# High weights on both input halves in one 512-column matmul, for the gate and up projections of a two-layer macaron encoder

## The reference, cut to what matters

```python
def swiglu(x, w_gate, w_up, w_down):
    return (jax.nn.silu(x @ w_gate) * (x @ w_up)) @ w_down

for l in range(DEPTH):                      # DEPTH = 2
    x = x + 0.5 * swiglu(rms_norm(x, ffn1_norm[l]), ...)   # 1024 -> 2816 -> 1024
    ...                                     # attention, gated recurrence, S5 on one projection
    x = x + 0.5 * swiglu(rms_norm(x, ffn2_norm[l]), ...)
```

## Time and profile before

| | |
|---|---|
| median of 3 runs (lowest to highest) | 1073.03 us (1072.99 to 1074.38) |
| the profiled execution's own time | 1073.09 us |
| its span in the trace | 1071.3 us |
| busy: PE / PEld / DVE / ACT / POOL | 98% / 96% / 61% / 47% / 20% |
| mean granted TensorE clock | 0.998 |
| the chain that ended last, PE's share | 90% |

### The profile page before, as it was taken

How to read it: one execution, slowest core, us unless ns; L and a number is a source line. 1 busy time by engine, 2 the same in 40 slices (tenths; PEclk the granted TensorE clock), 3 DMA queues, 4 the chain that set the end, 5 groups by cost and what they waited for, 6 DMA issues and landing times.

```text
span 1071.3 us, 21293 instructions
## 1 busy us (share of the span) xinstructions
PE 1053.6 (98%) x8990; PEld 1032.1 (96%) x8990; DVE 654.3 (61%) x807; ACT 505.5 (47%) x590; POOL 210.4 (20%) x296
## 2 busy tenths in 40 slices
PE   8899999999999999999999999999999999999998
PEld 7899999999988999999999999999998899999998
DVE  4567666788743556555566666667976355555554
ACT  5555434555543743343464743347445445434332
POOL 3005998100000100000010089941000010000000
PEclk9999999999999999999999999999999999999999
DMA  7545455434222464555556445453432155455541
GB/s 291 214 157 196 162 198 189 158 120 158 84 114 92 184 232 161 196 170 187 192 180 232 170 183 182 171 196 119 159 119 80 79 196 197 164 191 188 184 175 40
DMA packets 26828, 178.37 MB, mean 167 GB/s; under 512 B 3120, under 2 KB 4144, under 8 KB 5776
## 3 DMA queue, kind: packets, MB, share of 16 engines
q1 hardware_dynamic: 25632, 173.03, 44.7%
q10 hardware_dynamic: 1008, 4.05, 1.1%
q0 software_dynamic: 128, 0.44, 0.1%
HBM read 176.46 MB, written 1.05 MB: 166 GB/s over the span
## 4 chain that ended last, share of the span: by engine, by line
PE 90%; DVE 4%; ACT 2%; DMA 1%; issue 1%; POOL 1%; SPq 0%; DVEq 0%; ACTq 0%; POOLq 0%
PE ps L786 26%; PE ps L787 26%; PE ps L788 26%; PE ps L1147 5%; PE ps L978 2%; DVE lo L1178 1%; ACT hi L556 1%; DMA raw<-stream 1%; PE ps L939 1%; POOL sumsq L413 1%; PE ps L1043 0%; PE ps L1039 0%; DVE sc L1559 0%; PE ps L1000 0%; SPq L340 0%
## 5 line engine op out<-in xcount | busy, mean ns | idle before, releaser
L1178 DVE TENSOR_TENSOR lo<-raw,hi 128x2048 fp32r<-128x2048 f32 x130 | 303.8, 2342 | 291.4 <-ACT hi L556 291.4
L786 PE MATMUL ps<-xg_hi,hi 128*128 128x256 f32 x1408 | 400.5, 284 | 5.2 <-DVE lo L1178 4.9
L787 PE MATMUL ps<-xg_lo,hi 128*128 128x256 f32 x1408 | 399.2, 283 | 0.0
L788 PE MATMUL ps<-xg_hi,lo 128*128 128x256 f32 x1408 | 399.1, 283 | 0.0
L556 ACT ACTIVATE hi<-raw 128x2048 fp32r<-128x2048 f32 x130 | 247.2, 1907 | 252.6 <-PE ps L788 220.6
L786 PEld LDWEIGHTS ps<-xg_hi,hi 128*128 128x128 f32 x1408 | 270.9, 192 | 5.9 <-DVE lo L1178 5.1
L787 PEld LDWEIGHTS ps<-xg_lo,hi 128*128 128x128 f32 x1408 | 271.0, 192 | 0.2
L788 PEld LDWEIGHTS ps<-xg_hi,lo 128*128 128x128 f32 x1408 | 271.0, 192 | 0.0
L786 PE MATMUL ps<-act_hi,hi 128*128 128x256 f32 x704 | 199.6, 284 | 4.1 <-DVE act_lo L1216 4.1
L787 PE MATMUL ps<-act_lo,hi 128*128 128x256 f32 x704 | 199.2, 283 | 0.0
L788 PE MATMUL ps<-act_hi,lo 128*128 128x256 f32 x704 | 199.2, 283 | 0.0
(11 more groups left out here) (298 smaller groups left out, 1285.0 us busy)
## 6 DMA issues: line engine op xcount, KB each, us to landing
raw<-stream SPq DMA_DIRECT2D x160, 1024.0 KB, 4.8
par<-params ACTq DMA_DIRECT2D x2, 1463.0 KB, 6.2
raw<-stream SPq DMA_DIRECT2D x8, 256.0 KB, 7.0
rows<-stream SPq DMA_DIRECT2D x2, 1024.0 KB, 6.9
x<-xT ACTq DMA_DIRECT2D x4, 256.0 KB, 6.3
out<-x SPq DMA_DIRECT2D x8, 128.0 KB, 2.0
con<-consts POOLq DMA_DIRECT2D x1, 321.5 KB, 6.6
mask<-masks POOLq DMA_DIRECT2D x1, 112.0 KB, 6.3
```

Source lines behind the costliest of these rows:

```text
L786: pe.matmul(acc, w_hi, a_hi, start=start, stop=False, skip_group_check=True)
L787: pe.matmul(acc, w_hi, a_lo, start=False, stop=False, skip_group_check=True)
L788: return pe.matmul(acc, w_lo, a_hi, start=False, stop=stop, skip_group_check=True)
L1178: v.tensor_tensor(lo[slot][:, :], raw[slot][:, :], hi[slot][:, :].bitcast(F32), ALU.subtract).then_inc(lo_written, 1)
```

## The change

`hi*xg_hi` and `hi*xg_lo` become one matmul of 512 columns on a joint tile `xg` that holds both halves side by side, so its 512 sums fill a bank: the first 256 columns are the high part, the last 256 the rest. `lo*xg_hi` stays a matmul of 256 columns and adds to the first half. Now a block's gate sums take banks 6 and 7 and its up sums banks 4 and 5, so there is one set, and step i waits for `gated(i)` to have read block i, where it waited for `gated(i-1)`. ACT copies the second halves out of PSUM (into `silu` and `act` as scratch), DVE adds them to the first halves and multiplies by `rstd` in place. Block 0 of each FFN keeps the old form in banks 4 and 5; so does down. The four pieces below are `gate_up` and `step` on PE, the head of ACT's `gated`, and DVE's `gated`.

```diff
-                def gate_up(half, n, slot, b, between=lambda: None):
+                def gate_up(n, slot, b, between=lambda: None):
                         for k in range(KT):
                             w = k * 256 + m * P
-                            last = three(bank(b + m)[:, half * T:(half + 1) * T], hi[slot][:, w:w + P],
-                                         lo[slot][:, w:w + P], xg_hi[:, k, :], xg_lo[:, k, :],
-                                         k == 0, k == KT - 1)
+                            pe.matmul(bank(b + m), hi[slot][:, w:w + P], xg[:, k, :, :].rearrange("p s t -> p (s t)"),
+                                      start=k == 0, stop=False, skip_group_check=True)
+                            last = pe.matmul(bank(b + m)[:, 0:T], lo[slot][:, w:w + P], xg_hi[:, k, :],
+                                             start=False, stop=k == KT - 1, skip_group_check=True)
...
-                    pe.wait_ge(gu_read, f * ITERS + i + 1)
-                    gate_up(0, n, 2, 4 + 2 * g, lambda: row_sums(norm, False, 3) if head and first else None)
-                    gate_up(1, n + 1, 0, 4 + 2 * g)
+                    pe.wait_ge(gu_read, f * ITERS + i + (1 if first else 2))
+                    gate_up(n, 2, 6, lambda: row_sums(norm, False, 3) if head and first else None)
+                    if first:
+                        pe.wait_ge(gu_read, f * ITERS + i + 2)
+                    gate_up(n + 1, 0, 4)
...
+                    if folded:
+                        e.wait_ge(units_done, n0 + i * 3 + 1 + RING)
+                        e.wait_ge(act_lo_ready, f * ITERS + i)
+                        for b, rest in ((6, silu), (4, act)):
+                            e.activation(rest[:, :, :], bank(b, 2).rearrange("p (m s t) -> p m s t", m=2, s=2)[:, :, 1, :],
+                                         ACT.Copy).then_inc(rest_copied, 1)
...
+                    v.wait_ge(rest_copied, (f * (ITERS - 1) + i) * 2 - 1)
+                    v.tensor_tensor(gate[:, :, :], of_gate[:, :, 0, :], silu[:, :, :], ALU.add
+                                    ).then_inc(gate_summed, 1)
+                    v.wait_ge(rest_copied, (f * (ITERS - 1) + i) * 2)
+                    v.tensor_tensor(up[:, :, :], of_up[:, :, 0, :], act[:, :, :], ALU.add).then_inc(gu_read, 1)
+                    v.wait_ge(gate_summed, f * (ITERS - 1) + i)
+                    v.tensor_tensor(gate[:, :, :], gate[:, :, :], wide, ALU.mult).then_inc(gate_scaled, 1)
+                    v.wait_ge(gu_read, f * ITERS + i + 2)
+                    v.tensor_tensor(up[:, :, :], up[:, :, :], wide, ALU.mult).then_inc(up_scaled, 1)
```

More of the change, by code:

```diff
@@ L158, in build @@
         lo = [sb(f"lo{s}", [P, 2048], F32R, ffn_mem) for s in range(2)]
-        xg_hi = sb("xg_hi", [P, KT, T], F32R, ffn_mem)
-        xg_lo = sb("xg_lo", [P, KT, T], F32R, ffn_mem)
+        xg = sb("xg", [P, KT, 2, T], F32R, ffn_mem)
+        xg_hi, xg_lo = xg[:, :, 0, :], xg[:, :, 1, :]
         hi.append(sb("hi2", [P, 2048], F32R, ffn_mem))
@@ L268, in build @@
         gu_read = sem("gu_read")
+        gate_summed = sem("gate_summed")
+        up_scaled = sem("up_scaled")
+        rest_copied = sem("rest_copied")
         silu_done = sem("silu_done")
@@ L568, in ffn_steps, with gated @@
             def ffn_steps(f, n0, v0, ahead, between=lambda: None, later=lambda: None):
-                def gated(i, odd, after_silu=lambda: None, first=False):
+                def gated(i, odd, after_silu=lambda: None, first=False, folded=True):
+                    if folded:
[4 more added lines that the diff above has]
+                                         ACT.Copy).then_inc(rest_copied, 1)
                     e.wait_ge(gate_scaled, f * ITERS + i + 1)
@@ L582, in split_three @@
                     split_hi(n0 + i * 3 + 7, v0 + i + 2, 1)
-                gated(0, 0, first=True)
+                gated(0, 0, first=True, folded=False)
                 split_hi(n0 + 4, v0 + 1, 1)
@@ L1201, in boundary, with gated @@
                     rest_of_x(f, KT - 1, gain)
-            def gated(f, i, g, n_up, norm, after_act=lambda: None):
-                both = bank(4 + 2 * g, 2).rearrange("p (m s t) -> p m s t", m=2, s=2)
+            def gated(f, i, g, n_up, norm, after_act=lambda: None, first=False):
                 wide = rstd[:, :].unsqueeze(1).broadcast_to([P, 2, T])
@@ L1208, in gated @@
                 v.wait_ge(units_done, n_up + 1 + RING)
-                v.tensor_tensor(gate[:, :, :], both[:, :, 0, :], wide, ALU.mult).then_inc(gate_scaled, 1)
-                v.tensor_tensor(up[:, :, :], both[:, :, 1, :], wide, ALU.mult).then_inc(gu_read, 1)
+                if first:
+                    both = bank(4, 2).rearrange("p (m s t) -> p m s t", m=2, s=2)
+                    v.tensor_tensor(gate[:, :, :], both[:, :, 0, :], wide, ALU.mult).then_inc(gate_scaled, 1)
+                    v.tensor_tensor(up[:, :, :], both[:, :, 1, :], wide, ALU.mult).then_inc(gu_read, 1)
+                else:
+                    of_gate = bank(6, 2).rearrange("p (m s t) -> p m s t", m=2, s=2)
+                    of_up = bank(4, 2).rearrange("p (m s t) -> p m s t", m=2, s=2)
+                    v.wait_ge(rest_copied, (f * (ITERS - 1) + i) * 2 - 1)
[7 more added lines that the diff above has]
+                    v.tensor_tensor(up[:, :, :], up[:, :, :], wide, ALU.mult).then_inc(up_scaled, 1)
+                    v.wait_ge(up_scaled, f * (ITERS - 1) + i)
                 v.wait_ge(silu_done, f * ITERS + i + 1)
-                v.wait_ge(gu_read, f * ITERS + i + 2)
+                if first:
+                    v.wait_ge(gu_read, f * ITERS + i + 2)
                 v.tensor_tensor(act[:, :, :], silu[:, :, :], up[:, :, :], ALU.mult).then_inc(act_ready, 1)
@@ L1227, in ffn_steps @@
                 split_lo(n0 + 3, 0)
-                gated(f, 0, 0, n0, norm)
+                gated(f, 0, 0, n0, norm, first=True)
                 split_lo(n0 + 4, 1)
```

## The result

The changed kernel takes 1363.6 us (median of 4, 1360.5 to 1365.1) against 1073.45 us for the kernel before (4 runs). The ratio is 1.270, with an interval from 1.267 to 1.272: 290 us slower. The forecast was 1337.3 us, 26 us too low. The profiled execution took 1363.21 us, its span 1361.4 us.

A forecast was written before the change was run, and what follows sets the result against it. PE's matmul time bounds the kernel (90% of the chain of waits). 1073.1 + 208.8 (stalls) + 14.2 (S5 work less act_lo waits) - 12.8 (matmuls) + 54 (clock) = 1337.3 us; range 1285 to 1385.

The forecast's parts named there:

- The stall: Start of each step but an FFN's first: PE waits 5.8 us for DVE's sums, 36 times, 208.8 us.
- the two long gaps in FFN 0: S5 work between lo and two reads lengthens PE's gaps to 10.8 and 9.9 us; with FFN 2, 18.3 us added.
- ACT's copies and DVE's extra work: Copies run beside DVE's lo, added multiplications come after the release: 0 us; far end for slower copies +57.
- The waits for act_lo: Before down, PE starting later no longer waits for act_lo: all 4.1 us in 5 waits go.
- one chain with little cover: End of an FFN: chain of about 5.8 us beside down's 5.76; nothing, or tenths of a us four times.
- The matmuls: Gate and up: a pair takes 0.35 us where three matmuls took 0.36; 1280 triples save 12.8 us.
- the third rival: The stall comes and a matmul of 512 columns takes 216 ns: 1319.4 us; chance 17%.
- The clock: PE's clock falls after each of 36 stalls for 3.4 us, 45% lost, 1.5 us each: 54 us.
- harmless gap of 2.61 us: In the trace of before, a PE gap of 2.61 us cost no clock, taken as too short for a fall.
- rival 2: The stall comes but PE's clock holds: 1283.3 us; chance 12%.
- rival 4: The stall comes and the clock stays low 6.0 us after each, 97.2 us in place of 54: 1380.5 us; chance 13%.
- rival 1: PE never waits at a step's start, since the sums are ready at the start of down: 1060.3 us; chance 3%.

The follow-up runs named there:

- e4_wait_alone: Kernel before, with only PE's wait for gu_read at the start of a step asking for one block more: 1368.6 us, ratio 1.274.
- e1_reads_first: Changed kernel with DVE's and ACT's lists reordered, gated(i+1) ahead of the splits of slots 0 and 1: 1067.2 us, ratio 0.9935.
- e7_gate_read_only: Changed kernel, PE waiting at step start only for the gate half's sum, and for the up half's before writing those banks: 1335.8 us, ratio 1.244.

## Why the prediction was right, and what was off

**The stall: right.** Place, releaser, count and size are as forecast; of the two long gaps in FFN 0, named as 10.8 and 9.9 us, the first came out at 10.4. From down's last start to the first start of the next step the 36 steps of the trace take 231.8 us in sum. Less 0.12 each that is 227.5, against 208.8 + 18.3 = 227.1. e4_wait_alone shows the wait as the cause, e1_reads_first the order of the lists, e7_gate_read_only the last link of the chain.

**ACT's copies and DVE's extra work: right.** Copies of 0.58 us, hidden with 1.3 us to spare.

**The waits for act_lo: a bit off.** I took back the whole 4.1 us, of which 1.7 came. The wait at the end of FFN 1, 2.4 us, is new: there is the "one chain with little cover", with the next FFN's split in it, which I had not counted. I had called it tenths of a us.

**The matmuls: right.** 12.8 us were forecast. In the changed kernel a pair at full clock takes 0.351 us on average (0.232 and 0.117 at the median), a triple before took 0.361: 10 ns, 12.8 us. That it came out so well is partly luck, since the 0.23 us came from three starts in the warm-up, and with the better lists the saving is smaller (7.0 us from run to run). The 0.216 us of the plain fp32 rows is not reached (the median is 0.232, the least 0.224): the third rival, 1319.4 us, is out.

**The clock: the mechanism right, the term too small.** This is the term furthest off. Of the 290.2 us, 227.5 are stalls, -1.7 the waits for act_lo and -12.8 the matmuls; that leaves 77.2 for the clock, where I had 54. The difference to the forecast, 26.3 us, is 23.2 (clock) + 2.4 (act_lo) + 0.4 (stalls) + 0.3 (the median of before). The trace bears the 77 out. From PE's start behind a wait to the end of the low level it has 166 us, and 45% of it is 75, of which the kernel before had 1.5 already. The other 3 to 4 us are the slow first matmul of each stall (0.59 us to the next start in place of 0.43), which the forecast has nowhere.

The share lost of the low time, 45%, was right. What was wrong is the length. I took the 3.4 us of the one fall in the trace. Behind the 36 stalls it was 4.3 us on average, from 2.8 to 6.2. My reason for a harmless gap of 2.61 us was wrong too: that it was too short for a fall is not what the filled stalls show. It did little harm to the number, since all 36 stalls were longer; two falls behind gaps of 2.78 and 2.44 us, 6.6 us of low level, are within the 166.

**The rivals.** The clock didn't hold (rival 2) and didn't stay low for 6.0 us behind each stall (rival 4); rival 1 has the mechanism of e1_reads_first, a kernel with other lists; even that took 1067.2 us, not 1060.3.

## What to carry to other kernels

When a change takes away a second buffer, look for the instruction that frees the remaining one, and for what stands ahead of it on its engine's list; here it stood behind a split that waited for PE itself, so PE waited for its own last unit plus 4.35 us of other work and the two reads. The idle time of a buffer in the old trace (11.4 us here) against the time that PE spends elsewhere (5.76) told the stall before any run. An engine's stalls are paid for twice where its clock falls behind them; one fall in a trace gives no average, so take the range of lengths and not the one row. When a new form and a new order come together, run the order alone on the old kernel as well: here it was half of the gain.

## What the runs showed of the hardware

- Work without use in the stalls made the kernel 63 us faster (1363.6 to 1300.5 us), since the clock stayed at its higher level (0.986 against 0.906 in the mean).
- Gaps of 2.7 us were mostly followed by a fall (30 of 34 in one run), sometimes only after PE was back at full pace. Of the same gap in FFN 0, seven traces show a fall and four none.
- The first matmul of 512 columns behind a stall takes longer to the next start than those that follow: 0.59 against 0.43 us at the lower level, 0.33 against 0.23 at full clock.
- Loading the high weights once instead of twice and sending 512 columns through them saves 7 to 10 ns of a triple's 361 at full clock, though a third of the weight loads goes, and nothing at the lower clock (0.640 us both). A float32r matmul of 512 columns next to one of 256 takes 0.232 to 0.236 us at full clock (medians of two runs), where two plain fp32 matmul records of 256 columns lie 0.216 us apart.
